# Delta rule on one core: wider loads of the per-tile data, and the keys' factor moved from the key matrix to the residual

## The reference

```python
lower = where(strict, beta * kk * decay, 0) + eye          # kk = k k^T, decay = exp(gc_i - gc_j)
u, w = triangular_solve(lower, [v * beta, k * beta * exp(gc)])
qk, q_dec = (q k^T) * decay, q * exp(gc)
k_tail, g_tot = k * exp(gc[-1] - gc), exp(gc[-1])
def step(s, xs):                                           # chunk after chunk
    v_new = u_c - w_c @ s
    o_c = qd_c @ s + qk_c @ v_new
    s = s * gt_c + kt_c^T @ v_new
```

## Time and profile before

| | us |
|---|---|
| three runs | 3799.37, 3775.93, 3805.12 (median 3799.37) |
| the profiled execution | 3786.45 |
| its span in the profile | 3784.6 |
| mean granted clock of PE, as a share | 0.953 |

### The profile page before, as it was taken

How to read it: one execution, slowest core, us unless ns; L and a number is a source line. 1 busy time by engine, 2 the same in 40 slices (tenths; PEclk the granted TensorE clock), 3 DMA queues, 4 the chain that set the end, 5 groups by cost and what they waited for, 6 DMA issues and landing times. The chain is left out here.

```text
span 3784.6 us, 68890 instructions
## 1 busy us (share of the span) xinstructions
PE 3476.5 (92%) x26734; PEld 2979.7 (79%) x26734; DVE 2118.8 (56%) x4012; ACT 1362.6 (36%) x2626; POOL 1028.3 (27%) x1315
## 2 busy tenths in 40 slices
PE   7999999969999999994788569999976999999999
PEld 7999999957877788883777557888865888888887
DVE  6777777638978776932334336666654323233232
ACT  5544554433223232111455406666643111111111
POOL 4222222148988444300577600000000000000000
PEclk9999999989999999996798869999988999999999
DMA  5333333345347444335988222222246111121210
GB/s 158 107 104 111 108 112 107 86 133 179 93 128 213 136 138 121 102 99 118 231 244 248 68 65 96 71 85 72 84 152 224 67 60 67 60 72 59 67 67 35
DMA packets 322211, 429.81 MB, mean 114 GB/s; under 512 B 188587, under 2 KB 206283, under 8 KB 317310
## 3 DMA queue, kind: packets, MB, share of 16 engines
q1 hardware_dynamic: 321926, 425.94, 38.0%
HBM read 268.23 MB, written 160.25 MB: 113 GB/s over the span
## 5 line engine op out<-in xcount | busy, mean ns | idle before, releaser
L88 PE MATMUL b_psP<-b_w_hi,b_xT_hi 128*128 128x512 f32 x1320 | 518.8, 393 | 47.1 <-DVE b_xT_lo L1188 30.1
L89 PE MATMUL b_psP<-b_w_lo,b_xT_hi 128*128 128x512 f32 x1320 | 516.6, 391 | 0.0
L90 PE MATMUL b_psP<-b_w_hi,b_xT_lo 128*128 128x512 f32 x1320 | 516.2, 391 | 0.0
L88 PE MATMUL a_psG<-a_xT_hi,a_w_hi 128*128 128x256 f32 (+1 forms) x1632 | 467.8, 287 | 10.3 <-DVE a_xT_lo L559 9.4
L90 PE MATMUL a_psG<-a_xT_hi,a_w_lo 128*128 128x256 f32 (+1 forms) x1632 | 459.6, 282 | 0.0
L89 PE MATMUL a_psG<-a_xT_lo,a_w_hi 128*128 128x256 f32 (+1 forms) x1632 | 459.5, 282 | 0.0
L88 PEld LDWEIGHTS b_psP<-b_w_hi,b_xT_hi 128*128 128x128 f32 x1320 | 249.6, 189 | 105.7 <-DVE b_xT_lo L1188 53.8
L88 PEld LDWEIGHTS a_psG<-a_xT_hi,a_w_hi 128*128 128x128 f32 x1632 | 309.3, 189 | 26.2 <-DVE a_xT_lo L559 9.8
L576 DVE SCALAR_TENSOR_TENSOR a_act<-a_raw,a_taps,a_act 128x256 f32<-128x256 f32 x576 | 308.6, 536 | 20.5
L90 PEld LDWEIGHTS a_psG<-a_xT_hi,a_w_lo 128*128 128x128 f32 x1632 | 309.6, 190 | 0.0
L89 PEld LDWEIGHTS a_psG<-a_xT_lo,a_w_hi 128*128 128x128 f32 x1632 | 309.5, 190 | 0.0
(11 more groups left out here) (376 smaller groups left out, 7398.5 us busy)
## 6 DMA issues: line engine op xcount, KB each, us to landing
rows_b<-b_rows SPq DMA_DIRECT2D x165, 256.0 KB, 2.2
b_x_full<-xT SPq DMA_DIRECT2D x78, 512.0 KB, 4.0
qkvB<-a_act SPq DMA_DIRECT2D x16, 1536.0 KB, 5.1
d_conv_T<-qkvB SPq DMA_DIRECT2D x16, 1536.0 KB, 11.5
xT<-a_x_full SPq DMA_DIRECT2D x33, 512.0 KB, 5.1
h_mixed<-mixed SPq DMA_DIRECT2D x33, 512.0 KB, 4.0
out<-h_y SPq DMA_DIRECT2D x33, 512.0 KB, 2.9
a_x<-in_x_prompt SPq DMA_DIRECT2D x32, 512.0 KB, 4.6
```

The costliest lines, as they stand in the source:

```text
L88: nc.tensor.matmul(out, x_hi, w_hi, start=first, stop=False)
L89: nc.tensor.matmul(out, x_hi, w_lo, start=False, stop=False)
L90: return nc.tensor.matmul(out, x_lo, w_hi, start=False, stop=last)
```

## The change

`kqrow` becomes two tensors, `krow` and `qrow`, written at the same places (L978, L982). The factor of the key is no longer applied to the keys: POOL makes only `Qd`, and `keys_state` multiplies the raw keys of `conv_T` with the state. The key's factor comes as eight more rows of `rows` (now 24), is turned with the others (now into `psA` and `psB`, two copies to `scal`), negated once into `key_gain`, one number per frame and head, and DVE forms the residual as `psS * key_gain + vt`, one instruction of 64x64 for each head, four for each half. The loads of a tile become three beside `za`: two of `sc`, one for each chunk, that write 128 partitions (64 copies of one row for each half), and one of `UQ` over 128 partitions (LOADS = 3). `load_raw` also waits for `t_sk`, since `keys_state` now reads `conv_T`.

```diff
@@ -975,11 +975,11 @@
                         sp.wait_ge(v_rows, 3 * (n + 1))
-                        for x, there in ((krow, d.kqrow[:, :, 0]), (ketr, d.ketr)):
+                        for x, there in ((krow, d.krow), (ketr, d.ketr)):
                             sp.dma_start(there[chunks].rearrange("n h i -> (n h) i"), x[:, :]).then_inc(sc_out, 16)
                     elif kind == "seg":
                         sp.wait_ge(s_init, 1)
-                        sp.dma_start(d.kqrow[:, :, 1].rearrange("(g n) h i -> (n h) g i", g=GROUPS), egl).then_inc(eg_out, 16)
+                        sp.dma_start(d.qrow.rearrange("(g n) h i -> (n h) g i", g=GROUPS), egl).then_inc(eg_out, 16)
                         with nc.allow_non_contiguous_dma(reason="one decay per chunk and head, once"):
@@ -1418,7 +1418,7 @@
-    LOADS = 4
+    LOADS = 3
@@ -1432,14 +1432,14 @@
         UQ = some("UQ", [P, H, 2, C])
-        sc = some("sc", [P, 2, PAIRS, 2, C])
-        rows = ph.sb("d_rows", [2 * H, s.SEQ])
+        sc = some("sc", [P, 2, PAIRS, C])
+        rows = ph.sb("d_rows", [3 * H, s.SEQ])
         za = some("za", [P, W], ZBUFS)
-        Kd = some("Kd", [P, PAIRS, P], 2)
         Qd = some("Qd", [P, PAIRS, P], 2)
         kt = some("kt", [P, W], 2)
         vt = some("vt", [P, W], 2)
-        scal = ph.sb("d_scal", [P, NT, 2 * H])
+        scal = ph.sb("d_scal", [P, NT, 3 * H])
+        key_gain = ph.sb("d_key_gain", [P, NT, H])
         S = some("S", [P, PAIRS, C], 2)
@@ -1472,9 +1472,9 @@
+        v_key = ph.sem("d_v_key")
-        g_kd = ph.sem("d_g_kd")
@@ -1523,6 +1523,7 @@
                     sp.wait_ge(g_qd, 2 * (x - 2))
+                    sp.wait_ge(t_sk, 2 * 2 * 2 * (x - 2))
                 sp.dma_start(conv_T[x % 3][:, :, :], d.qkvB[x]).then_inc(conv_in[x % 3], 16)
@@ -1531,11 +1532,12 @@
                 ok = c_in[b]
-                for e in range(2):
-                    half = slice(e * C, (e + 1) * C)
-                    sp.dma_start(sc[b][half, :, :, :, :],
-                                 d.kqrow[2 * t:2 * t + 2, e * PAIRS:(e + 1) * PAIRS].partition_broadcast(C)).then_inc(ok, 16)
-                    sp.dma_start(UQ[b][half, :, :, :], d.UQ[:, 2 * t + e]).then_inc(ok, 16)
+                for c in range(2):
+                    sp.dma_start(sc[b][:, c, :, :].rearrange("p a i -> p (a i)"),
+                                 d.qrow[2 * t + c].rearrange("(e a) i -> e (a i)", e=2).unsqueeze(1)
+                                 .to_broadcast([2, C, PAIRS * C])).then_inc(ok, 16)
+                sp.dma_start(UQ[b][:, :, :, :].rearrange("p h x i -> p (h x i)"),
+                             d.UQ[:, 2 * t:2 * t + 2].rearrange("j e h x i -> e j (h x i)")).then_inc(ok, 16)
                 if t >= ZBUFS:
@@ -1551,6 +1553,8 @@
                     sp.dma_start(rows[H:2 * H, :], d.ssqT).then_inc(rows_in, 16)
+                    sp.dma_start(rows[2 * H:3 * H, :].rearrange("h (c i) -> h c i", i=C), d.krow.rearrange("c h i -> h c i"))\
+                        .then_inc(rows_in, 16)
             for t in range(NT):
@@ -1585,10 +1589,9 @@
                     g.wait_ge(t_qs, 2 * 2 * (t - 1))
-                for out_, x, first, done in ((Kd, 0, PAIRS, g_kd), (Qd, 1, 0, g_qd)):
-                    g.tensor_tensor(out_[t % 2][:, :, :].rearrange("p a (c i) -> p c a i", c=2),
-                                    raw(t)[:, first:first + PAIRS, :].rearrange("p a (c i) -> p c a i", c=2),
-                                    sc[b][:, :, :, x, :], ALU.mult).then_inc(done, 1)
+                g.tensor_tensor(Qd[t % 2][:, :, :].rearrange("p a (c i) -> p c a i", c=2),
+                                raw(t)[:, 0:PAIRS, :].rearrange("p a (c i) -> p c a i", c=2),
+                                sc[b][:, :, :, :], ALU.mult).then_inc(g_qd, 1)
 
@@ -1699,10 +1702,8 @@
                 pe.wait_ge(v_state, 2 * n + x + 1)
-                if x == 0 and n % 2 == 0:
-                    pe.wait_ge(g_kd, t + 1)
                 for p, e, h, at, rows_e in half_heads(x):
-                    last = nc.tensor.matmul(psS[x][c, e, p - 2 * x, :], Kd[t % 2][rows_e, p, c], old[rows_e, p, :],
+                    last = nc.tensor.matmul(psS[x][c, e, p - 2 * x, :], raw(t)[rows_e, PAIRS + p, c], old[rows_e, p, :],
                                             start=True, stop=True)
@@ -1741,11 +1742,13 @@
 
-            pe.wait_ge(rows_in, 32)
+            pe.wait_ge(rows_in, 48)
             for t in range(NT):
-                last = nc.tensor.transpose(psA[:, t * 2 * H:(t + 1) * 2 * H], rows[:, t * P:(t + 1) * P], ident[0:2 * H, 0:2 * H])
+                to = (psA, psB)[t // (NT // 2)]
+                at = t % (NT // 2) * 3 * H
+                last = nc.tensor.transpose(to[:, at:at + 3 * H], rows[:, t * P:(t + 1) * P], ident[0:3 * H, 0:3 * H])
             last.then_inc(t_rows, 1)
-            pe.wait_ge(v_scal, 1)
+            pe.wait_ge(v_scal, 2)
             prepare(0)
@@ -1786,9 +1789,14 @@
                         v.wait_ge(t_tr, 2 * (n - 2) + x + 1)
-                    v.tensor_tensor(r[c, at].rearrange("p (a e c) -> p e a c", a=2, e=2),
-                                    vt[t % 2][c, at].rearrange("p (a e c) -> p e a c", a=2, e=2), psS[x][c, :, :, :],
-                                    ALU.subtract).then_inc(v_r, 1)
+                    for a in range(2):
+                        for e in range(2):
+                            p = 2 * x + a
+                            cols = slice((2 * p + e) * C, (2 * p + e + 1) * C)
+                            h = e * PAIRS + p
+                            op = v.scalar_tensor_tensor(r[c, cols], psS[x][c, e, a, :], key_gain[c, t, h:h + 1], vt[t % 2][c, cols],
+                                                        ALU.mult, ALU.add)
+                    op.then_inc(v_r, 1)
 
@@ -1807,9 +1815,14 @@
             v.wait_ge(t_rows, 1)
-            v.tensor_copy(scal[:, :, :].rearrange("p t h -> p (t h)"), psA[:, 0:NT * 2 * H]).then_inc(v_scal, 1)
-            v.wait_ge(v_scal, 1)
-            v.tensor_scalar(floor[:, :, :], scal[:, :, H:], C * EPS, C * EPS * EPS, ALU.mult, ALU.add).then_inc(v_floor, 1)
+            part = NT // 2
+            for i, src in enumerate((psA, psB)):
+                v.tensor_copy(scal[:, i * part:(i + 1) * part, :].rearrange("p t h -> p (t h)"), src[:, 0:part * 3 * H])\
+                    .then_inc(v_scal, 1)
+            v.wait_ge(v_scal, 2)
+            v.tensor_scalar(floor[:, :, :], scal[:, :, H:2 * H], C * EPS, C * EPS * EPS, ALU.mult, ALU.add).then_inc(v_floor, 1)
+            v.tensor_scalar(key_gain[:, :, :], scal[:, :, 2 * H:], -1.0, None, ALU.mult).then_inc(v_key, 1)
+            v.wait_ge(v_key, 1)
             keys(0)
@@ -3207,7 +3220,7 @@
-    d.kqrow = scratch("kqrow", [NCH, s.HA, 2, s.DV])
+    d.krow, d.qrow = (scratch(k, [NCH, s.HA, s.DV]) for k in ("krow", "qrow"))
```

## The result

The changed kernel takes 4137.02 us (median of 4, 4132.56 to 4142.85) against 3802.24 us for the kernel before (median of 4): a ratio of 1.0894, 95% interval 1.0837 to 1.0950. The forecast was 4135. The profiled execution has a span of 4130.8 us.

The account below looks back on a forecast made before the run. It took the delta stage's compute chain, slowed by competing transfers, as the bound. With loads on two engines, 1774 + 6 + 669 + 35 put the stage's end at 2484 us, +352 on 3786; forecast 4135 us, range 4040 to 4330.

Parts of the forecast that it names:

- The cut along the outermost count: Delta stage loads: transfers are split over engines by outermost count, so each of the three loads uses two engines.
- The price of two engines: Delta stage: each of two engines needs 20.9 us per tile, against 8.44 for compute; 669 us for 32 tiles.
- The tail: End of the delta stage, after the last load: 35 us of compute left, bounds 20.6 and 46.
- The stage: The delta stage as a whole: ends at 2484 instead of 2132 us, +352 us.
- The residual: DVE in the delta stage, four instructions per half: +0.4 us a chunk, +26 us on the chain, hidden but for the tail.
- The stalls of before: Delta stage of the kernel before: 325 us window against 270 at compute pace, some 55 us of stalls while DMA is full.
- rival (a): Delta stage loads spread over 16 engines and the stalls go: -38 us, 3748 us; chance 0.04.
- (b): Delta stage loads spread, about half of the stalls stay, residual at +26: 3785 us, no change; chance 0.05.
- (c): Delta stage loads spread, DVE takes the chain with four instructions without overlap, +71 - 28: 3829 us; chance 0.04.
- Signs: Delta stage profile if right: DMA share about 0.25, about 100 GB/s, 46 small packets a tile, PE waiting for `d_UQ` or `d_sc`.

Follow-up runs that it names:

- spread64: The changed kernel with only its loads taken back to two DMAs of 64 partitions each for `d_sc` and `d_UQ`; 3797.13 us, ratio 0.9975 to the kernel before.
- wide: The changed kernel with 128-partition loads whose two sides both begin with 128, reading other rows, same bytes; 3795.40 us, ratio 0.9987 to the kernel before.
- before_uq_two: The kernel before with only `d_UQ` loaded in the changed shape, source 2 outermost; 4047.80 us, executed once.
- uq_two: The changed kernel with only `d_UQ` left in the changed shape, `d_sc` spread over 64 partitions and 16 engines; 4001.37 us, executed once.
- before_half_sc: The kernel before with `d_sc` halved, both factors read from `ketr`, so values differ; 3760.28 us, ratio 0.9907 to the kernel before.
- before_wide: The kernel before, all bytes kept, with `d_sc` and `d_UQ` loaded over 128 partitions from sources beginning with 128, other rows; 3767.81 us, ratio 0.9917.
- one_residual: `spread64` with one 64x256 residual instruction per half instead of four of 64x64, values differ; 3773.03 us, ratio 0.9913 to the kernel before.

## Why the prediction was right

- *The cut along the outermost count* carried the forecast, and it holds: 42.6 small packets a tile after, 104.6 with the loads taken back, and the whole 340 us goes with it (`spread64`, `wide`, `before_uq_two`). The rule that the Trainium skill states ("DMA: Bandwidth & Descriptors", why a DMA increments its semaphore by 16 and not by 1) agrees with sides of 2 and 128, which no row of before showed.
- *The price of two engines*: 20.9 us a tile forecast, about 20.1 measured, tiles of 18.2 to 21.1 by turns. The rates from the earlier trace rows held: a packet of 4 KiB took 175 ns in the mean from 1850 to 2050 us, 23 GB/s, where it took 312 in the kernel before. That this is because 14 engines idle is argued, not tested. `uq_two` (15.5 for 15.8) bears out the term of `d_UQ` by itself.
- *The tail*: 35 us taken, 44 measured: the last packet of 4 KiB ends at 2432.5 and the stage at 2476.8. The mechanism, compute one to three tiles behind the loads because of the store, was right: at 2432.5 the third tile from the end is under way, and POOL still waits 2 us for a store. Both terms were short. PE turns the last tile's keys at 2452.5, 20.0 us after the last load (14.4 taken: two tiles less a part, at 8.44), and the stage ends 24.3 us after that (20.6 taken).
- *The stage*: +352 forecast, +324.6 measured. 32 tiles at 0.8 us less make -26, the longer tail +9, and the rest, -10, is the start: I had put 9 us before the first tile's loads, for a first transfer and for constants, but the whole way from the stage's first instruction to the last packet of 4 KiB is 641.6 us, which 32 tiles of 20.1 fill. The total agreed within 6 us of the profiled execution only because `project_a` was 20.6 us shorter in the profile of before. The forecast of the stage was 27 us too high; that the total came within 2 us of the measured median is chance.
- *The residual*: I took 0.4 us a chunk, 26 us if bare, with bounds of 0.25 and 1.1. With the loads out of the way it is 1.10 us a tile, 0.55 a chunk; over a third more than the value, inside the bounds. The bounds were loose: two small instructions start 0.20 us apart, where I took 0.13 at best although my own reading of the row gave 0.2, and the terms that I named (0.72 us for each half, less the 0.7 that PE covers) make 0.74 at most and not 1.1. Under the loads it was hidden but for the tail, as said.
- *The stalls of before*: I read 325 - 270 = 55 us, and the paces agree: from the first residual of the stage (1799.3 us) to that of the last tile (2117.3) are 318.0 us, 56 more than 31 tiles at 8.44. But relief of the DMAs gives back only 36 or 37 (`before_half_sc`, `before_wide`), so rival (a), 3748 us, would have been wrong by its own sum even where its condition holds. It holds in `spread64` and `wide`: there the tiles are only 10 and 6 us above 31 times 9.54, but 9.54 for 8.44 takes 34 us, and they came to 3797 and 3795 us. That lies between (b) and (c), and (c)'s mechanism, DVE on the chain, is the better description of it, as `one_residual` shows.
- *Signs*: share of 0.25 forecast, 0.32 measured; the 14 engines are busier than I made them. 100 GB/s forecast, 103 measured; 46 small packets a tile forecast, 42.6 measured; four residual instructions in 0.7 to 1.1 us forecast, 1.62/2 = 0.81 measured. The trace shows no landing for `d_UQ` and `d_sc`, so whether each lands tens of us after its issue is not known; the spread loads beside them take 17 to 20. That PE would wait for `d_UQ` or `d_sc` was wrong: it waits for POOL, and POOL for the store.

## What to carry to other kernels

Before a load is merged to fill 128 partitions, write down the outermost count of both sides: a source that begins with 2 put the whole transfer on two engines, and here nearly doubled the stage. Count the small packets of a tile, and see whether a transfer that is spread lands late: both show it in one look. Do not take the store that everybody waits for as the cause before you know what stands ahead of it in its queue. And where a chain waits for a few instructions, one instruction over several heads was worth more than one for each head: move the per-head factor to where it is off the chain, as the norm was.

## What was not expected of the hardware

SP is held in its issues while the engines that it issues to are behind. Its timeline in the changed kernel (start, us, queue, line):

```profile
2120.88 12.17 SPq L1536 DMA_DIRECT2D d_sc<-qrow  x1
2133.11 4.29 SPq L1539 DMA_DIRECT2D d_UQ<-UQ  x1
...
2145.85 8.60 SPq L1539 DMA_DIRECT2D d_UQ<-UQ  x1
...
2157.74 0.99 SPq L1527 DMA_DIRECT2D d_conv_T<-qkvB  x1
```

One issue took 12.17 us here and up to 14.4 in the stage, while that of the spread `d_conv_T` behind them took 0.99. It isn't that such an issue is long in itself: the stage's first `d_sc`, with the engines still free, took 0.59 us, as much as one in the kernel before. From 1850 to 2400 us SP is inside an issue for 534 of 550 us. So the store behind them is late twice: for tiles 8 to 23, SP issues it 23.4 us after POOL's product in the mean (6.6 in `spread64`), and it lands 15.2 us after its issue (4.8). More of the lateness is SP's queue than the engines'.

Small DVE instructions on PSUM follow one another at 1.62/8 = 0.20 us, though each lasts 286 ns: they overlap, yet four of 64x64 are still busy for twice as long as one of 64x256 (106.8 us in the stage for 49.0 to 56.5). A busy engine moved a quarter more where loads covered 128 partitions at once (21.5 against 16.9 GB/s). It isn't the size of the pieces: from 1850 to 2050 us a packet of 4 KiB took 312 ns in the mean in the kernel before and 211 in `before_wide`. Ports are one explanation; larger transfers in smaller number, or the other rows of DRAM that `before_wide` reads, are others, and no run here tells them apart.
